# State table of an S5 scan laid out chunk-innermost, x loaded in scan order by two queues

## What is computed

```python
xr = einsum('ntgc,gpc->ntgp', ug, bbr); xi = einsum('ntgc,gpc->ntgp', ug, bbi)   # 64 groups of 16 channels, 64 states
h[t] = lambda * h[t-1] + x[t]                                                    # complex, per group and state
y = einsum('ntgp,gcp->ntgc', hr, c_re) - einsum('ntgp,gcp->ntgc', hi, c_im)
y = gelu(y + d_skip * uf); z = y @ w_glu; out = z[..., :D] * sigmoid(z[..., D:])
```

## Time and profile before

| | us |
|---|---|
| median of 3 runs | 2776.86 |
| lowest, highest run | 2776.39, 2782.03 |
| span of the profiled execution, first to last instruction | 2777.0 |
| TensorE busy in it | 2657.4 (96%) |
| VectorE, ScalarE, GpSimd busy | 1364.9, 843.2, 265.2 |
| mean granted clock of TensorE | 0.979 |

### The profile page before, as it was taken

One profiled execution on the slowest core, in us unless ns is written; L12 is line 12 of the kernel. 1 busy time (PEld: TensorE's weight loads), 2 busy tenths in 40 slices (PEclk: granted clock), 3 DMA queues, 4 the chain that ended last, 5 costly groups with the idle time before them and its releaser, 6 DMA issues.

```text
span 2777.0 us, 44438 instructions
## 1 busy us (share of the span) xinstructions
PE 2657.4 (96%) x18594; PEld 2535.8 (91%) x18594; DVE 1364.9 (49%) x2262; ACT 843.2 (30%) x1703; POOL 265.2 (10%) x433
## 2 busy tenths in 40 slices
PE   5589999999999999999999999979999999999999
PEld 4479999999999999988888888856999999999998
DVE  7982235433333332866666767676364333233325
ACT  6232122211221122335455455464131112111213
POOL 2200000000000000013142522430000000000000
PEclk7789999999999999999999999999999999999999
DMA  3511111111111111232234545397111111111101
GB/s 99 82 38 56 45 37 47 45 46 46 45 45 45 45 45 46 102 81 72 75 85 121 132 120 133 77 329 265 46 46 46 46 45 45 45 45 45 45 31 63
DMA packets 176832, 205.14 MB, mean 74 GB/s; under 512 B 48679, under 2 KB 130967, under 8 KB 176426
## 3 DMA queue, kind: packets, MB, share of 16 engines
q1 hardware_dynamic: 150242, 154.48, 18.7%
q0 software_dynamic: 19776, 43.87, 5.8%
q10 hardware_dynamic: 6672, 4.82, 0.8%
HBM read 156.74 MB, written 27.69 MB: 66 GB/s over the span
## 4 chain that ended last, share of the span: by engine, by line
PE 80%; DVE 6%; issue 2%; ACT 2%; POOL 1%; DMA 1%; ACTq 0%; DVEq 0%
PE PS L221 12%; PE PS L217 12%; PE PS L218 12%; PE PS L417 9%; PE PS L414 9%; PE PS L413 9%; PE PS L2306 4%; PE PS L2307 3%; PE PS L2308 3%; PE PS L2337 2%; PE PS L2364 2%; PE PS L2351 1%; DVE SSB L2230 1%; DMA CB<-C_SCRATCH 1%; DVE SQ L191 1%
## 5 line engine op out<-in xcount | busy, mean ns | idle before, releaser
L217 PE MATMUL PS<-XH,WH 128*128 128x352 f32 x1920 | 617.3, 322 | 4.0 <-PEq L103 3.8
L218 PE MATMUL PS<-XL,WH 128*128 128x352 f32 x1920 | 618.9, 323 | 0.0
L414 PE MATMUL PS<-HIDL,WH 128*128 128x352 f32 x1524 | 490.7, 323 | 0.0
L413 PE MATMUL PS<-HIDH,WH 128*128 128x352 f32 x1524 | 489.4, 322 | 0.0
L221 PE MATMUL PS<-XH,WL 128*128 128x352 f32 x1920 | 414.9, 324 | 0.0
L217 PEld LDWEIGHTS PS<-XH,WH 128*128 128x128 f32 x1920 | 362.1, 189 | 4.6 <-issue 4.5
L218 PEld LDWEIGHTS PS<-XL,WH 128*128 128x128 f32 x1920 | 361.0, 188 | 0.1
L354 DVE TENSOR_TENSOR H<-PS,H 128x1056 f32<-128x1056 f32 x127 | 159.6, 1257 | 397.7 <-PE PS L417 397.4
L221 PEld LDWEIGHTS PS<-XH,WL 128*128 128x128 f32 x1920 | 329.4, 188 | 0.0
L417 PE MATMUL PS<-HIDH,WL 128*128 128x352 f32 x1524 | 329.0, 324 | 0.0
L331 DVE TENSOR_TENSOR TMP<-TMP 128x1056 f32<-128x1056 f32 x64 | 80.6, 1259 | 472.5 <-ACT TMP L294 472.3
(11 more groups left out here) (401 smaller groups left out, 3409.2 us busy)
## 6 DMA issues: line engine op xcount, KB each, us to landing
RAW<-w_up SPq DMA_DIRECT2D x32, 1024.0 KB, 5.4
RAW<-w_down SPq DMA_DIRECT2D x32, 1024.0 KB, 4.9
KVR<-cache_kv_w SPq DMA_DIRECT2D x18, 1024.0 KB, 11.9
QB<-QA SPq DMA_DIRECT2D x120, 132.0 KB, 2.6
ARAW<-w_q SPq DMA_DIRECT2D x24, 512.0 KB, 4.8
O_SCRATCH<-OT POOLq DMA_DIRECT2D x96, 128.0 KB, 3.0
OB<-O_SCRATCH POOLq DMA_DIRECT2D x24, 512.0 KB, 7.2
RAW<-w_glu SPq DMA_DIRECT2D x16, 512.0 KB, 4.8
```

What stands on the lines that cost most here:

```text
L217: nc.tensor.matmul(out, wh(k), xh[:, k, c], start=(k == 0), stop=False)
L218: nc.tensor.matmul(out, wh(k), xl[:, k, c], start=False, stop=False)
L413: nc.tensor.matmul(out, w, m.hidh[:, k, q], start=(k == 0), stop=False)
L414: nc.tensor.matmul(out, w, m.hidl[:, k, q], start=False, stop=False)
```

## The change

Chunk number n = 8 s + i (segment s, place i in the segment) now lives in row and column 16 i + s. The state table `XS` becomes [re/im, q, column]: the 128 columns of one state lie side by side, and column block i holds the state before the chunk at place i. The states at the segments' ends get a table of their own, `ENDS`, in the place of `CRI`.

```diff
-        self.xs = at("XS", [128, NCH + 1, 2, NQ], F32, XS_AT)
+        self.xs = at("XS", [128, 2, NQ, NCH], F32, XS_AT)
+        self.ends = at("ENDS", [128, NSEG, 2, NQ], F32, CRI_AT)
...
-    def states(self, lo):
-
-        return self.xs[:, lo:lo + NCH].rearrange("p (s i) a q -> p s i a q", i=SEG)
+    def states(self, i, lo=0):
+
+        return self.xs[:, :, :, NSEG * i + lo:NSEG * i + NSEG]
...
+    def load_rows(eng, odd):
+
+        for part in range(2):
+            ts = slice(L // 2 * part, L // 2 * part + L // 2)
+            for i in range(odd, SEG, 2):
+                eng.dma_start(s.xt[NSEG * i:NSEG * i + NSEG, ts, :], x_scan[i, :, ts]).then_inc(f.x_in[part], 16)
+
+    def y_turned(k):
+
+        return ps[:, 2 * (k % 3):2 * (k % 3) + 2, :].rearrange("p b (t i s) -> p (b t) s i", i=SEG, s=NSEG)
+
+    def by_token(x, k):
+
+        return x[:, k, 0:SEQ].rearrange("p (t s i) -> p t s i", t=L, i=SEG)
...
-            act.wait_ge(f.x_in[t // 2], 32)
+            act.wait_ge(f.x_in[2 * t // L], 16 * SEG)
...
-            nc.scalar.activation(s.xs[:, 1:NCH + 1, :, 2 * p:2 * p + 2], v[:, 0:NCH], ACT.Copy)
+            nc.scalar.activation(xv[:, :, :, NSEG:NCH], v[:, :, :, 0:NCH - NSEG], ACT.Copy)
+            nc.scalar.activation(xv[:, :, :, 0:NSEG], v[:, :, :, NCH - NSEG:NCH], ACT.Copy)
...
-                nc.scalar.activation(m.xh[:, k - 1, 0:SEQ], bank4(2 * ((k - 1) % 3), 2), ACT.Copy).then_inc(f.x_hi, 1)
+                nc.scalar.activation(by_token(m.xh, k - 1), y_turned(k - 1), ACT.Copy).then_inc(f.x_hi, 1)
...
-        step(nc.vector.memset(s.xs[:, 0], 0.0))
...
+                dve.wait_ge(f.k_done, 4)
+                nc.vector.tensor_tensor(s.ends[:].rearrange("p s a q -> p a q s"), y, tt[:, 1, ::-1], ALU.add).then_inc(f.local, 1)
...
+        nc.vector.memset(s.xs[:, :, :, 0], 0.0)
+        step(nc.vector.tensor_copy(s.states(0, 1), s.ends[:, 0:NSEG - 1].rearrange("p s a q -> p a q s")))
...
-            nc.vector.tensor_tensor(m.xl[:, k, 0:SEQ], bank4(2 * (k % 3), 2), f32(m.xh[:, k, 0:SEQ]), ALU.subtract).then_inc(f.x_lo, 1)
+            nc.vector.tensor_tensor(by_token(m.xl, k), y_turned(k), f32(by_token(m.xh, k)), ALU.subtract).then_inc(f.x_lo, 1)
...
-                        mm = nc.tensor.matmul(ps[:, 2 * (k % 3) + r, 128 * x:128 * x + 128], s.xs[half, 0:NCH, i, q],
+                        mm = nc.tensor.matmul(ps[:, 2 * (k % 3) + r, 128 * x:128 * x + 128], s.xs[half, i, q, :],
```

More of the change, by code:

```diff
@@ L660, in __init__ @@
         self.lam_seg = at("LAM_SEG", [128, 2, 2, NQ], F32, SMALL_AT + 1312)
-        self.xtmp = at("XTMP", [128, NSEG, 2, 2, NQ], F32, H_AT + 4096)
+        self.xtmp = at("XTMP", [128, 2, 2, NQ, NSEG], F32, H_AT + 4096)
         self.ct = at("CT", [128, 2, 2, NQ], F32, WT_AT)
-        self.cc = [at(f"C{i}", [128, NSEG - 1, SEG // 2, NQ // 2], F32, RAW_AT + 8192 + 4096 * i) for i in range(2)]
+        self.cc = [at(f"C{i}", [128, SEG // 2, NQ // 2, NSEG], F32, RAW_AT + 8192 + 4096 * i) for i in range(2)]
         self.h0 = at("H0", [128, 2, NS, NQ], F32, SMALL_AT + 1824)
@@ L700, in __init__ @@
         self.nc, self.m, self.s = nc, m, s
-        self.x_in = [sig(f"x_in{i}") for i in range(4)]
+        self.x_in = [sig(f"x_in{i}") for i in range(2)]
         (self.ident_in, self.row_in, self.b_in, self.c_in, self.h_in, self.gain_in, self.g_in, self.smp_in, self.set0) = (
@@ L731, in s5_phase @@
     xp = a["x_prompt"][0].rearrange("(p t) d -> p t d", p=128)
+    x_scan = a["x_prompt"][0].rearrange("(s i t) d -> i s t d", i=SEG, t=L)
     xs_rows = a["x_sample"].rearrange("n t d -> (n t) d")
@@ L761, in _ @@
         sp.dma_start(s.sxt[:], a["x_sample"]).then_inc(f.smp_in, 16)
-        for t in range(L):
-            sp.dma_start(s.xt[:, t, :], xp[:, t, :]).then_inc(f.x_in[t // 2], 16)
+        load_rows(sp, 1)
         sp.wait_ge(f.t_zero, 1)
@@ L1122, in _ @@
         step(nc.vector.tensor_scalar(s.lam_seg[:, 1, 1], s.pt[:, 1, SEG - 1, :], -1.0, None, ALU.mult))
-        dve.wait_ge(f.s_turned, 1)
-        step(nc.vector.memset(s.xs[:, 0], 0.0))
         dve.wait_ge(f.inc_kept, NQ // 2)
-        after, tt = s.states(1), s.xtmp
+        tt = s.xtmp
+        lam = bc(s.lam[:].rearrange("p b a q -> p b (a q)"), 3, NSEG)
         for i in range(1, SEG):
[L1129 to L1133, removed]
+            x, y = s.states(i), s.states((i + 1) % SEG)
+            step(nc.vector.tensor_tensor(tt[:].rearrange("p b a q s -> p b (a q) s"), lam,
+                                         bc(x.rearrange("p a q s -> p (a q) s"), 1, 2), ALU.mult))
+            step(nc.vector.tensor_tensor(y, y, tt[:, 0], ALU.add))
             if i < SEG - 1:
-                step(ins)
-        ins.then_inc(f.local, 1)
+                step(nc.vector.tensor_tensor(y, y, tt[:, 1, ::-1], ALU.add))
+            else:
+                dve.wait_ge(f.k_done, 4)
+                nc.vector.tensor_tensor(s.ends[:].rearrange("p s a q -> p a q s"), y, tt[:, 1, ::-1], ALU.add).then_inc(f.local, 1)
         dve.wait_ge(f.local, 1)
         dve.wait_ge(f.s_state, 1)
[L1139 to L1143, removed]
+        for j in range(NSEG - 1):
+            step(nc.vector.tensor_tensor(s.ct[:], s.lam_seg[:], bc(s.ends[:, j], 1, 2), ALU.mult))
+            step(nc.vector.tensor_tensor(s.ends[:, j + 1], s.ends[:, j + 1], s.ct[:, 0], ALU.add))
+            ins = nc.vector.tensor_tensor(s.ends[:, j + 1], s.ends[:, j + 1], s.ct[:, 1, ::-1], ALU.add)
+            if j < NSEG - 2:
                 step(ins)
@@ L1172, in _ @@
             for part, (lo, n) in enumerate(((0, SEG // 2), (SEG // 2, SEG // 2 - 1))):
-                c0, c1 = (s.cc[j][:, :, 0:n] for j in range(2))
-                carry = [bc(s.states(0)[:, 1:NSEG, 0, j, qs], 2, n) for j in range(2)]
-                pw = [bc(s.pt[:, j, lo:lo + n, qs], 1, NSEG - 1) for j in range(2)]
+                c0, c1 = (s.cc[j][:, 0:n, :, 1:NSEG] for j in range(2))
+                carry = [bc(s.states(0, 1)[:, j, qs], 1, n) for j in range(2)]
+                pw = [bc(s.pt[:, j, lo:lo + n, qs], 3, NSEG - 1) for j in range(2)]
                 for j, op in enumerate((ALU.subtract, ALU.add)):
-                    x = after[:, 1:NSEG, lo:lo + n, j, qs]
+                    x = s.xs[:, j, qs].rearrange("p q (i s) -> p i q s", s=NSEG)[:, lo + 1:lo + 1 + n, :, 1:NSEG]
                     nc.vector.tensor_tensor(c0, carry[0], pw[j], ALU.mult)
@@ L1366, in _ @@
         for i in range(2):
-            tr(ps[0:NQ, 6, 128 * i:128 * i + 128], s.xs[:, NCH, i, :], m.ident[:])
+            tr(ps[0:NQ, 6, 128 * i:128 * i + 128], s.ends[:, NSEG - 1, i, :], m.ident[:])
             for j in range(2):
```

6 lines of the change are left out of this document (4 added, 2 removed).

## The result

The changed kernel takes 2803.36 us (median of 4 runs, 2801.33 to 2805.66), the kernel before 2777.76 (4 runs): the ratio is 1.0088, with a 95% interval from 1.0076 to 1.0100. It is slower by 25.6 us; the forecast was 2774.6, and its range ended at 2781.0. The profiled execution's span is 2803.2 us, 26.2 more than before. S5 ends 26.8 us late (246.49 in place of 219.67), and what stands behind it takes 0.6 us less, so all of the loss lies in S5.

The account below looks back on a forecast made before the run. TensorE, 96% busy, was taken to bound the kernel; only the first 220 us could move, where engines wait in turn. −1.2 + 0 + 0 − 2.0 + 0.9 = −2.3 from 2777.0, as median 2774.6; range 2769.8 to 2781.0.

Parts of the forecast that it names:

- part 1: Load of x at the start, 16 KB rows, half on ScalarE's queue: −1.2 us, between 4.7 gained and 2.2 late.
- lands no earlier than now: Worst case for the load of x: first half lands at 19.81, squares end at 31.28, 2.2 us late.
- Rival C: Loads of 16 partitions are slower, two at a time reaching half of 424 GB/s: up to +2.2, 2776.8 us; chance 0.10.
- signs that I had named: Included first square before 17.6 and S5's end near 217.4; wrong if S5 ends more than 5 us from 219.67.
- ScalarE's issues: At the start, eight DMA issues on ScalarE cost 4.73 us, beside its wait of 6.05 before the first square.
- parts 2 and 3: `keep_increments` (0.8 us more) and VectorE's scan with `ENDS` (0.6 to 3.7 more), both covered by waits: 0 each.
- part 4: L1380 in S5's output blocks, loads side by side: 1.9 us per block in place of 3.76, −2.0 on the path.
- rival E: The load does not pace L1380, so part 4 is 0: 2776.6 us; chance 0.12.
- rival A: TensorE's new idle time in S5's tail lowers its clock for k = 7: +4.3 us, 2778.9; chance 0.20.
- part 5: L989 and L1156 read PSUM one element in 16: ten times 0.09 us on the path, +0.9.
- rival B: PSUM reads with steps cost double, VectorE and ScalarE bound the tail: 2784.9 us; chance 0.12.

Follow-up runs that it names:

- d1_one_queue: c2_neighbours with all sixteen DMAs of x (16 neighbouring partitions x 16 KB) issued by SP on one queue; 2807.5 us.
- c2_neighbours: c1_turned_u with x loaded in the changed kernel's shape: sixteen DMAs of 16 neighbouring partitions x 16 KB on two queues; 2802.4 us.
- c1_turned_u: Changed kernel with x loaded as before the change, the new column order made in the copies of turned U out of PSUM; 2779.53 us, ratio 1.0001.

## Why the prediction was wrong

**The load (part 1).** This is the step that failed: "4.7 us gained at most" and "2.2 us late" were the bounds, −1.2 the value; it was +28.1. I reasoned about when a transfer could start (ScalarE's early issue) and took its rate for the 424 GB/s of the earlier trace rows. That rate was measured on DMAs of 128 partitions and is no property of the engines. The bound "lands no earlier than now" was no bound at all: nothing in the profile before showed a load of x to 16 partitions. Rival C named the mechanism, but sized it at half of 424 by letting two queues' DMAs count as 32 partitions. d1_one_queue and c2_neighbours show that the second queue adds next to nothing (125 and 129 GB/s). And it reckoned as if only x were slow: the packets of POOL's loads, 4 KB to many partitions, took a median of 0.51 us in place of 0.17 while x was loading, so that `CST` landed at 51.8 too. Of the signs that I had named one came at once: S5 ended more than 5 us from 219.67.

Rows of the kernel before did hint at it. `T` is filled by DMAs that write 16 neighbouring partitions each, and that stretch reads (share, GB/s at the end):

```profile
120.00:140.00 20.00, 8.00 (x150) 7.43 (x151) 19.55 (x14) 4.62 (x9) 2.71 (x5) 0.51 1.11 156
```

Full engines at 156 GB/s, 56 of them POOL's loads of 4 KB to 128 partitions. With 512 B and less in a packet for `T` it proves nothing, but it should have put the lower end of rival C near a third of 424, not at half.

**ScalarE's issues.** Eight of them took 4.45 us (4.73 predicted), and lay beside a wait, as said. What they do to other loads the prediction left out. ScalarE's x came ahead of the small parameters that SP loads, and VectorE, which starts on them at 4.67 before and at 4.68 in d1_one_queue, where SP issues all of x, had to wait in the kernel after:

```profile
24.84 0.21 DVE L1024 COPY AROW<-LDT 32x128 f32<-32x128 f32 x1 [23.24 <-DMA DGR<-norm_mix]
```

These 20 us lay beside the wait for x. What they would cost with a faster load issued by ScalarE was not measured.

**The increments and the scan (parts 2 and 3).** Right. The two copies for a pair take 545 + 218 = 763 ns, 125 more than L894's 638 (100 predicted). The write of `ENDS` takes 1.98 us in place of 1.22 (0 to 1.2 more predicted), the new copy of 960 elements 0.97, in the range of 0.6 to 2.3; the correction went on with 0.77 us of slack left of 3.42, so 0 on the path.

```profile
L911 ACT ACTIVATE XS<-PS 128x448 f32<-128x448 f32 x16 | 8.7, 545 | 4.3 <-PE PS L1282 3.2
L912 ACT ACTIVATE XS<-PS 128x64 f32<-128x64 f32 x16 | 3.5, 218 | 0.0
```

**L1380 (part 4).** The mechanism and the size were right: the load paces the pair, and side by side it goes as fast as L1323's. Loads of L1401 in the kernel after (count, ns min/median/max, starts), beside 308 in the earlier trace rows:

```profile
L1401 PEld LDWEIGHTS PS<-W,XS x256: 182/188/335, 201.6 to 241.3; 64*128 64x128 f32 x128
```

A block of 32 takes 2.06 us (1.9 predicted, 3.76 before), so rival E falls. But the −2.0 on the path did not come: rival A did, with its mechanism and about half of its size. `take_u` of k = 7 took 3.65 us after and 3.78 in c1_turned_u ("about 4.0"), the block of L1380's successor behind it 2.06 and 3.08 ("3.7"), and the two turns were not slower. That is 1.8 and 2.9 us of A's 4.3. I had given it 0.20 and counted "less than a third of a block's" idle time against it; that was not enough to keep the clock.

**Reading PSUM with steps (part 5).** +0.9 forecast, 0 measured. These are L989's and L1156's successors, which read one element in 16, beside 1005 and 1217 ns before; so rival B falls, and what the prediction cites for it from the Trainium skill does not hold for these reads, where the measurement decides:

```profile
L1175 DVE TENSOR_TENSOR XL<-PS,XH 128x1024 fp32r<-128x1024 f32 x8 | 9.7, 1218 | 0.0
...
L1008 ACT ACTIVATE XH<-PS 128x1024 fp32r<-128x1024 f32 x8 | 8.0, 1005 | 0.0
```

Without the load, the sum would have been 0 (c1_turned_u against before: 2779.5 and 2779.2), against a forecast of −1.1 for those parts, inside what a measurement can tell from no change. Two terms of that forecast were wrong and partly cancel, the −2.0 that the clock took back and the +0.9 that the stepped reads did not cost, so that its closeness is luck.

## What to carry to other kernels

Before reshaping a load, ask how many different partitions are written at one time, and price it by a row of the same shape; a rate measured on 128 partitions says nothing about sixteen. An operation that gets shorter on TensorE is a gain only if the idle time behind it doesn't cost the clock of the next one that lies on the path: look at the granted clock there, and cost the next block at both levels.

## What the runs showed that I had not expected

- A source whose outermost dimension is 8 uses only half of the DMA engines' time (share 0.50 to 0.51 in three kernels). With rows of 4 KB the packets are as fast as ever (208 GB/s in place of 403), with 16 KB they are slower too (134 in place of 384).
- With 16 neighbours and 16 KB, two queues carry hardly more than one (129 and 125 GB/s), and either way POOL's packets of 4 KB to other partitions become about three times as long (a median of 0.17 us before, 0.51 after, 0.49 in d1_one_queue).
- Runs of 4 KB to 16 neighbours were faster than runs of 16 KB (x landed at 43.4 in place of 51.6; 219 GB/s for a while, 101 with one queue left). Why is open; that DMAs of several queues, to different sets of partitions, overlap better with short runs would fit, and wasn't tried.
- ScalarE and VectorE read PSUM one element in 8 or in 16 at no cost (604 to 620 ns for the copies of U with steps, 618 without; 1005 and 1218 ns for the two above).
